# One backbone layer pair on one Trainium2 core: which engine copies the delta rule's turned blocks, when the scan's first products may start, and how far attention's transposes lag

## What is computed

```python
# attention of one differential head
s = einsum('bqhmd,bthmd->bhmqt', dq, dk) * ATTN_SCALE
p = softmax(s)
a = p[:, :, 0] - lam * p[:, :, 1]
d_out = rms_norm(einsum('bhqt,bthe->bqhe', a, dv), subln_g) * (1 - lam_init)
# delta rule, per chunk and head
m = where(strict, (kb @ k.T) * decay, 0)
tmat = triangular_solve(eye + m, eye)          # inverse of a unit lower triangle
u, w = tmat @ vb, tmat @ (kb * exp(gcum))
# scan over the chunks
v_new = u - w @ S
o = (q * exp(g)) @ S + ((q @ k.T) * dec) @ v_new
S = S * exp(g_last) + (k * exp(g_last - g)).T @ v_new
```

## Time and profile before

| what | value |
|---|---|
| median of 3 runs | 1274.23 us (1273.56 to 1274.49) |
| profiled execution | 1275.03 us |
| its span in the profile | 1273.3 us |
| mean granted TensorE clock | 0.973 |
| PE busy | 1185.7 us |
| DVE, ACT, POOL busy | 598.5, 558.5, 118.7 us |

### The profile page before, as it was taken

How to read it: one execution, slowest core, us unless ns; L and a number is a source line. 1 busy time by engine, 2 the same in 40 slices (tenths; PEclk the granted TensorE clock), 3 DMA queues, 4 the chain that set the end, 5 groups by cost and what they waited for, 6 DMA issues and landing times.

```text
span 1273.3 us, 18814 instructions
## 1 busy us (share of the span) xinstructions
PE 1185.7 (93%) x7613; PEld 953.1 (75%) x7613; DVE 598.5 (47%) x942; ACT 558.5 (44%) x1027; POOL 118.7 (9%) x110
## 2 busy tenths in 40 slices
PE   5899988889889999999999899999889997999996
PEld 2577734458468888888888568788789876999996
DVE  2532266662453233233222475589855525545444
ACT  2622345663462222223222376665465435444542
POOL 0030220100001101111000000010015100111000
PEclk9899999999999999999999999999879997999998
DMA  9645555572463333333333453235003042666560
GB/s 344 208 155 157 169 186 186 198 148 83 132 165 99 93 93 96 99 95 91 92 98 105 136 149 83 67 83 130 3 20 84 20 133 79 183 182 183 168 181 34
DMA packets 239393, 159.60 MB, mean 125 GB/s; under 512 B 14778, under 2 KB 213836, under 8 KB 239308
## 3 DMA queue, kind: packets, MB, share of 16 engines
q1 hardware_dynamic: 238528, 158.11, 42.6%
q10 hardware_dynamic: 780, 0.29, 0.1%
HBM read 157.33 MB, written 1.05 MB: 124 GB/s over the span
## 4 chain that ended last, share of the span: by engine, by line
PE 81%; DVE 9%; ACT 5%; issue 2%; DMA 1%; SPq 1%; POOL 1%; DVEq 0%; ACTq 0%; POOLq 0%
PE bank L1364 57%; PE bank L1391 3%; PE bank L1351 2%; PE bank L1441 2%; PE bank L1534 2%; PE bank L1422 1%; PE bank L775 1%; PE bank L1544 1%; DVE blocks L1027 1%; DVE outer L1025 1%; ACT h_work L1666 1%; DMA w_raw<-in_ada_w 1%; PE bank L1565 1%; PE bank L778 1%; PE bank L773 1%
## 5 line engine op out<-in xcount | busy, mean ns | idle before, releaser
L1364 PE MATMUL bank<-h_hi,w_hi 128*128 128x512 f32 (+1 forms) x976 | 349.7, 358 | 4.5 <-issue 4.5
L1838 DVE TENSOR_TENSOR w_lo<-w_raw,w_hi 128x1024 fp32r<-128x1024 f32 (+1 forms) x179 | 220.6, 1234 | 280.4 <-ACT w_hi L1633 280.0
L1364 PE MATMUL bank<-h_hi,w_lo 128*128 128x512 f32 (+1 forms) x976 | 345.3, 354 | 0.0
L1364 PE MATMUL bank<-h_lo,w_hi 128*128 128x512 f32 (+1 forms) x976 | 345.1, 354 | 0.0
L1633 ACT ACTIVATE w_hi<-w_raw 128x1024 fp32r<-128x1024 f32 (+1 forms) x179 | 184.0, 1031 | 79.2 <-PE bank L1364 73.9
L1364 PEld LDWEIGHTS bank<-h_hi,w_hi 128*128 128x128 f32 x976 | 184.6, 189 | 30.6 <-issue 5.2
L1364 PEld LDWEIGHTS bank<-h_hi,w_lo 128*128 128x128 f32 x976 | 184.6, 189 | 25.7
L1364 PEld LDWEIGHTS bank<-h_lo,w_hi 128*128 128x128 f32 x976 | 184.7, 189 | 25.1 <-issue 0.5
L1364 PE MATMUL bank<-act_lo,w_hi 128*128 128x512 f32 (+1 forms) x352 | 118.3, 336 | 0.0
L1364 PE MATMUL bank<-act_hi,w_hi 128*128 128x512 f32 (+1 forms) x352 | 118.3, 336 | 0.0
L1364 PE MATMUL bank<-act_hi,w_lo 128*128 128x512 f32 (+1 forms) x352 | 118.3, 336 | 0.0
(11 more groups left out here) (260 smaller groups left out, 1483.4 us busy)
## 6 DMA issues: line engine op xcount, KB each, us to landing
w_raw<-in_ada_w SPq DMA_DIRECT2D x96, 512.0 KB, 5.0
w_raw<-in_ffn_w_gate_up SPq DMA_DIRECT2D x88, 512.0 KB, 3.9
w_raw<-in_ffn_w_down SPq DMA_DIRECT2D x32, 512.0 KB, 3.9
w_raw<-in_gdn_w_in SPq DMA_DIRECT2D x32, 512.0 KB, 4.0
w_raw<-in_attn_w_in SPq DMA_DIRECT2D x14, 512.0 KB, 4.0
w_raw<-in_ffn_w_down SPq DMA_DIRECT2D x16, 384.0 KB, 3.5
w_raw<-in_gdn_w_out SPq DMA_DIRECT2D x8, 512.0 KB, 5.4
w_raw<-in_attn_w_in SPq DMA_DIRECT2D x8, 256.0 KB, 3.5
```

The costliest lines, as they stand in the source:

```text
L1364: m = nc.tensor.matmul(dst, stationary(a, k), moving(b, k), start=(first and k == kk[0] and a == b == 0), stop=(last and k == kk[-1] and a ...
L1838: nc.vector.tensor_tensor(w_lo[where[key] % N_RAW][:, 0:tiles, 0:w], raw_slot(key)[:, 0:tiles, 0:w], w_hi[m % N_SPLIT][:, 0:tiles, 0:w].bi ...
```

## The change

It has three parts.

1. ScalarE no longer copies `turned_blocks` to `turned` nor direction 1's `inverses` to `gram`. VectorE does: `turned_on(d)` at steps 31 and 32 of the loop, and `inverse_back()` behind it, four copies each of 32 partitions by 1024. ScalarE's copies of direction 0's inverses move from steps 28 and 29 to 31 and 32.
2. POOL clears the 64-wide blocks chunk by chunk, each behind its own Z64, and a product VN waits for its own chunk's clearing and T64 alone. The list has VN(0) behind Z64(3), then T64(2), S(0), T64(3). VN, S and the rest of the scan are otherwise as before.
3. In attention the transposes of a unit come three iterations behind its scores instead of two, its values four instead of three, and `probs` is a ring of four. All that hangs on these (the head's copies, the norm's places, now 8, 12, 16, 20) moves by one.

```diff
-        probs = at("probs", [3, 2, T], F32, BIG + 55296)
+        probs = at("probs", [PROB_RING, 2, T], F32, BIG + 55296)
...
-            jobs += [("T64", 0), ("Z64", 2), ("T64", 1), ("Z64", 3), ("T64", 2), ("T64", 3)]
-            jobs += scan_jobs(0, None, ("VN", "S"))
+            jobs += [("T64", 0), ("Z64", 2), ("T64", 1), ("Z64", 3)]
+            jobs += scan_jobs(0, None, ("VN",)) + [("T64", 2)] + scan_jobs(0, None, ("S",)) + [("T64", 3)]
...
                     elif kind == "VN":
-                        pe.wait_ge(cleared, 2)
-                        for cc in range(CHUNKS):
-                            wait_evacuated(pe, ("T64", d, cc))
                         wait_evacuated(pe, ("vt", GH - 1))
...
+                    if kind == "VN":
+                        pe.wait_ge(cleared, 2 + c)
+                        wait_evacuated(pe, ("T64", d, c))
...
-                if n in (INVERSE_AT + 1, INVERSE_AT + 2):
-                    inverse_back(act, 0, n - INVERSE_AT - 1)
+                if n in (JOIN_AT + 1, JOIN_AT + 2):
+                    inverse_back(act, 0, n - JOIN_AT - 1)
                 if n in (JOIN_AT, JOIN_AT + 1):
                     off_diagonals_out(act, n - JOIN_AT)
-                if n in (LAST - 1, LAST):
-                    inverse_back(act, 1, n - LAST + 1)
...
-                if kind == "T32" and job[1] == 0:
-
-                    for d in range(2):
-                        act.wait_ge(turned_in, d + 1)
-                        for half in range(2):
-                            part = rows(2 * d + half)
-                            last = nc.scalar.activation(turned[part, :, rows(half)], turned_blocks[d][part, :, :], ACT.Copy)
-                    last.then_inc(turned_ready, 1)
...
+            def turned_on(d):
+
+                dve.wait_ge(turned_in, d + 1)
+                for half in range(2):
+                    part = rows(2 * d + half)
+                    last = nc.vector.tensor_copy(turned[part, :, rows(half)], turned_blocks[d][part, :, :])
+                if d:
+                    last.then_inc(turned_ready, 1)
+
+            def inverse_back():
+
+                dve.wait_ge(inverse_in, 2)
+                for b in range(4):
+                    last = nc.vector.tensor_copy(gram[1][rows(b), :, rows(b)], inverses[1][rows(b), :, :])
+                last.then_inc(diagonal_ready, 2)
...
+                if n in (JOIN_AT + 1, JOIN_AT + 2):
+                    turned_on(n - JOIN_AT - 1)
+            inverse_back()
...
+            def clear_64(c):
+
+                units_of = slice(c * GH, (c + 1) * GH)
+                for d in range(2):
+                    wait_product(pool, ("Z64", d, c))
+                    part, cols = (slice(0, 64), slice(64, P)) if d else (slice(64, P), slice(0, 64))
+                    last = nc.gpsimd.memset(gram[d][part, units_of, cols], 0.0)
+                    if d == 0:
+                        link(last)
+                last.then_inc(cleared, 1)
+                pool.wait_ge(cleared, 2 + c)
...
-            clear(False)
-            clear(True)
+            clear_32()
+            for c in range(CHUNKS):
+                clear_64(c)
...
-                if 2 <= n < len(ATT_UNITS) + 2:
-                    turn(n - 2)
-                if 3 <= n < len(ATT_UNITS) + 3:
-                    values(n - 3)
+                if TURN_LAG <= n < len(ATT_UNITS) + TURN_LAG:
+                    turn(n - TURN_LAG)
+                if TURN_LAG < n <= len(ATT_UNITS) + TURN_LAG:
+                    values(n - TURN_LAG - 1)
...
-SUBLN_AT = [4 * h + 7 for h in range(DIFF_HEADS)]
+TURN_LAG, PROB_RING = 3, 4
+SUBLN_AT = [4 * h + 5 + TURN_LAG for h in range(DIFF_HEADS)]
```

More of the change, by code:

```diff
@@ L928, in gdn_scalar @@
                 kind = job[0]
-                if kind == "T32" and job[1] == 0:
-                    for d in range(2):
-                        act.wait_ge(turned_in, d + 1)
-                        for half in range(2):
-                            part = rows(2 * d + half)
-                            last = nc.scalar.activation(turned[part, :, rows(half)], turned_blocks[d][part, :, :], ACT.Copy)
-                    last.then_inc(turned_ready, 1)
-                elif kind == "Z64":
+                if kind == "Z64":
                     c = job[1]
@@ L1242, in gdn_gpsimd, with clear_32 @@
             last.then_inc(pads_ready, 1)
-            def clear(big):
+            def clear_32():
                 for d in range(2):
[L1247 to L1253, removed]
                     for q in range(2):
@@ L1261, in clear @@
                 last.then_inc(cleared, 1)
-                pool.wait_ge(cleared, 1 + big)
+                pool.wait_ge(cleared, 1)
+            def clear_64(c):
[8 more added lines that the diff above has]
+                pool.wait_ge(cleared, 2 + c)
             def decay_queries(d):
@@ L1569, in values @@
                 done_at[("o", tile)] = jobs[0]
-            for n in range(len(ATT_UNITS) + 4):
+            for n in range(len(ATT_UNITS) + TURN_LAG + 2):
                 if n < len(ATT_UNITS):
@@ L1781, in _ @@
                                                      accum_out=stats[:, n % 4, 2 + m:3 + m]), ("s", n, m))
-                if 3 <= n < len(ATT_UNITS) + 3 and ATT_UNITS[n - 3][1] == 3:
-                    tile = ATT_UNITS[n - 3][0]
+                if TURN_LAG < n <= len(ATT_UNITS) + TURN_LAG and ATT_UNITS[n - TURN_LAG - 1][1] == 3:
+                    tile = ATT_UNITS[n - TURN_LAG - 1][0]
                     src = bank(("o", tile))
@@ L1792, in _ @@
                     release(nc.scalar.activation(o_sb[:, tile, :], src, ACT.Copy), ("o", tile))
-                if 2 <= n < len(ATT_UNITS) + 2:
-                    tile, qb = ATT_UNITS[n - 2]
+                if TURN_LAG <= n < len(ATT_UNITS) + TURN_LAG:
+                    u = n - TURN_LAG
+                    tile, qb = ATT_UNITS[u]
                     for m in turned_maps(tile):
-                        job = ("t", n - 2, m)
+                        job = ("t", u, m)
                         wait_product(act, job)
-                        if n >= 4:
-                            wait_product(act, ("v", n - 4))
-                        release(nc.scalar.activation(probsT[:, (n - 2) % 2, m, 0:keys_of(qb) // P, :],
+                        if u >= 2:
+                            wait_product(act, ("v", u - 2))
+                        release(nc.scalar.activation(probsT[:, u % 2, m, 0:keys_of(qb) // P, :],
                                                      units(bank(job)[:, 0:keys_of(qb)]), ACT.Copy), job)
```

11 lines of the change are left out of this document (6 added, 5 removed).

## The result

The changed kernel takes **1263.99 us** (median of 4 runs, 1263.2 to 1265.35) against 1274.36 for the kernel before on the same chip: ratio **0.9916, interval 0.9905 to 0.9928**. Forecast were 1262.0 in a range of 1257.5 to 1269.5, so the direction and the range held, and the gain is 10.4 us where 12.2 were forecast. The profiled execution took 1263.31 with a span of 1261.6 and a mean clock of 0.977 (before: 1273.3, 0.973).

A forecast was written before the change was run, and what follows sets the result against it. TensorE, busy 93% of the span, was taken as the bound, so only its waits and clock could change. Attention -7.8 and hand-over -4.4 gave -12.2 us, from median 1274.23 to 1262.0; range 1257.5 to 1269.5.

The forecast's parts named there:

- The two 2.02 stalls: Attention: PE's two 2.02 us waits in transposes for VectorE's probabilities, each behind a head's norm, were to go.
- Attention's clock: Attention: the low-clock stretch at 215 to 219 us behind the second norm goes, -1.6 us; lower bound 0.
- (a): Hand-over: ScalarE's direction 0 copies no longer precede the last k_tok, so PE starts the 32-wide products earlier, -1.7 us.
- (b): Hand-over: ScalarE's moved copies free the banks for the first 32-wide join later, a new wait, +0.7 us.
- (c): Hand-over: VectorE's eight copies precede its evacuation of the first join, +0.2 us; +0.8 at most by the skill's port rule.
- (d): Hand-over: ScalarE loses 8.5 us of copies and gets 4.3 back elsewhere; PE did not wait for them, 0.
- (e): Hand-over: first VN waits only for its own chunk's memsets and T64; -3.8 + 1.9 for two later T64 = -1.9 us.
- (f): Hand-over: first VN, right behind Z64(3), runs at full clock, 5.47 against 3.74, -1.7 us; q7's clock taken as 0.
- The start of q7 is warm: Hand-over rival: q7's projection runs at full clock because the quiet stretch is shorter, -1.9 us more, 1260; chance 0.14.
- Half of attention's gain: Attention rival: new waits for probsT twice as long and low clock returns elsewhere, time 1266; chance 0.14.
- no gain from the hand-over: Hand-over rival: VectorE's copies cost +3.7 and VN's clock gain (1.7) is absent, time 1267; chance 0.10.
- the slower case: Attention rival: values' wait bounds each iteration without a modulation product, 14 us lost, time 1276; chance 0.05.

The follow-up runs named there:

- e5: Kernel before with only the norms moved to iterations 8, 12, 16, 20, lag two and ring of three kept; 1268.31 us, ratio 0.9949.
- e6: Changed kernel with the norms put back to iterations 7, 11, 15, 19, lag three and ring of four kept; 1273.88 us, ratio 0.9994.
- e1: Kernel before with part 3 alone (attention: lag of three, ring of four, norms one later); 1267.27 us, ratio 0.9944.
- e2: Kernel before with parts 1 and 2 alone (VectorE's copies, clearing and waiting by chunk); 1270.75 us, ratio 0.9972.
- e3: Kernel before with part 1 alone (VectorE's copies, ScalarE's copies later); 1274.02 us, ratio 0.9991.
- e8b: Changed kernel plus six filling products, results overwritten, in PE's idle time before the 32-wide products; 1260.81 us, ratio 0.9892.
- e10: Changed kernel with both e7's spread splits and e8b's six filling products; 1259.91 us, ratio 0.9886.
- e4: Kernel before with part 2 alone (POOL clears by chunk, VN waits for its own chunk); 1271.8 us, ratio 0.9969.
- e7: Changed kernel with the three output-weight splits at iterations 30, 31 and 32 instead of all at 32; 1262.79 us, ratio 0.9902.
- e8: Changed kernel plus twelve filling products, results overwritten, in PE's idle time before the 32-wide products; 1263.66 us, ratio 0.9910.
- e9: Changed kernel with VectorE's four 32x1024 copies out of the inverses done twice; 1268.42 us, ratio 0.9951.
- e11: Changed kernel itself timed and profiled once more, with more rounds; 1264.38 us, ratio 0.9920.

## Why the prediction was right, and where it was not

- **Attention's waits**: forecast 7.7 us left of 13.9, measured 7.6. The parts: end 2.9 (forecast 2.9), first values 1.26 (1.5), scores waiting for a bank 1.3 (0.7), small ones 2.1 (2.6). With the clock, attention measures -7.52 where -7.8 was forecast. Right in its size, **wrong in the reason that it gave for most of it**. "The two 2.02 stalls go: between the point where they stood and the new place of the same transpose lies one iteration of PE work" was the step; e5 has no such iteration between, and there they shrink to two of 0.9, with the same gain for the stage. The bank waits were put down to the lag too ("under lag 3 five banks are taken before bank 2 comes up again"), and they go in e5 at lag two and stand in e6 at lag three. The norm's place, which I took as an appendix of the lag, does both. The walk through the queues had both edits in it at once, so its sum could be right while its reading was not.
- **Attention's clock** (-1.6): the low stretch went, as forecast. But low clock came at the start of the output projection, +1.4, behind a wait of 2.53 that had been harmless before. That is the lower bound of the prediction ("a low stretch could come elsewhere"), and the largest single part of what is missing. It belongs to neither attention nor the change: in the 14 profiled runs these 8 us have 1.00 six times (before, e1, e2, e3, e8b, e10) and 0.79 to 0.82 eight times (e4, e5, e6, e7, e8, e9 and the changed kernel twice), always behind 2.53 or 2.54 us without work. e8b, whose program is the changed kernel's up to there, has this row:

```profile
279.63:287.63 8.00, 8.00 (x35) 6.65 (x36) 0.43 (x1) 2.25 (x4) 0.00 (x0) 1.00 0.14 32
```

- **(a)** wait before L618 2.7 forecast, 2.71 measured. **(b)** 0.7 forecast, 0.51 measured.
- **(c)** eight copies 0.7 to 0.9 each: 0.70 for the four out of the inverses, 5.00 for the four that meet POOL's memsets, whose four grew from 3.95 to 5.33. Taken one by one these four are 0.67, 1.43, 1.42 and 1.43, the first of them begun as the first memset ended; the memsets are 0.94 ahead of the copies and 1.38 to 1.45 beside them. The Trainium skill ("SBUF — State Buffer", Who interferes with whom) has the loser wait for the whole instruction, and the trace agrees: memsets end at 918.96, 920.39 and 921.83, copies at 919.51, 920.94 and 922.39, always in turn. The prediction's sum for that rule was too low: from -2.0 of slack at the low price (7.9 + 4.1 - 9.1 - 4.9) up to four waits of 0.99 lead to +2.0, not to +0.8; the copies' rows give 2.2 us of waiting on VectorE. PE paid nothing of it where +0.2 was forecast, but only because its row decays ran at low clock: 0.6 us of cover here, and 0.3 to 0.5 paid in e7 and e3, where they were quicker.
- **(d)** nothing, as forecast. **(e) and (f)** together -3.6, measured -3.7 from the start of KQ to KS, and here **the sum is better than its terms**. -3.7 holds KQ, 0.7 shorter by the clock, which was no term. (f), VN's clock, measures -1.6 of the forecast -1.7, but it was put down to the missing wait, and e3 and e5 have VN at full clock with the wait in place; that the kernel before was profiled with it low is in part luck. (e) is then -1.4 and not -1.9: the two T64 cost 1.08 each and not 0.9.
- **Missing in the hand-over**: -4.4 forecast, -3.4 measured. q7 stayed as cold as before (5.91 against 5.67), as I had it. The terms that I had (wait -1.67, join +0.51, chain 0, from KQ to KS -3.68) measure -4.8. Against them stand q7 (+0.24), PE's stop inside the first join, where nothing that the trace shows is waited for, of 2.18 and not 1.52 us (row at 924.16, +0.66), the row decays of 5.13 and not 4.92 (+0.21), and 0.3 in smaller rows. The stop inside the join was no term of the sum. At the scan's end -10.2 was reached of the -12.2: attention 0.3 short, the output projection 1.4, the hand-over 1.0 and the scan 0.1, against 0.8 gained by chance ahead of attention.
- **The rivals.** "The start of q7 is warm" (1260) is half true: it differs from run to run (3.72 in e2 and e7, 5.91 and 4.83 in the changed kernel), and e8b with its filling has it, at 1260.8. Half of attention's gain, no gain from the hand-over, the slower case (the values' wait as the bound of each iteration) and no change are refuted by e1, e2 and the 2.5 us that all L1575 waits make together.

## What to carry to other kernels

When an edit moves two things by one constant, move each alone before believing the story of the first: here a norm moved by one iteration gave attention's whole gain and the deeper ring next to none. A wait on "everything cleared" at the head of a long chain is worth splitting by piece, even if the pieces are paid for later: here two T64 of 1.1 us each moved behind the first products and about 1.4 us of gain were left, with 1.6 more where the wait had lowered the clock. And read two profiled runs of one program before calling a microsecond behind a 2 to 3 us wait a gain or a loss.

## What the hardware showed that I had not expected

- The same wait, behind the same instructions, leaves TensorE at its lower clock or not, by the run. Behind the 2.53 us before the output projection the clock was 1.00 in e8b and 0.82 and 0.79 in the changed kernel; behind the 2.7 us before the 32-wide products q7 took 3.72, 4.83, 4.84 and 5.91 in e7, e11, e9 and the changed kernel, whose programs are alike from the output projection to there; behind 1.24 us the first VN took 5.47 twice and 3.84 twice. With products in the gap of 2.7 it was 3.72 in three of three, without them in two of seven.
- VectorE's fp32 copies of 32x1024 within SBUF took 0.67 to 0.70 us alone and 1.43 beside POOL's memsets of the same shape, which went from 0.94 to 1.38 and more: the two ended strictly in turn.
- One product of two fp32 operands is two instructions in the trace (12 products, 24 instructions, 0.22 us each for 256 columns), which doubled the filling of e8.
- Inside each run of the 32-wide joins PE stands still once, 1.2 to 2.7 us in the first join (before 1.52, changed 2.18 and 2.36, e7 2.45) and 1.4 to 2.3 in the second, with no releaser in the trace. What it is was not tried and stays open; it is at least 3 us of every run.
